# Modulation tiles split differently between two FFNs, and token places dealt out to partitions in steps of four

## What is computed

```python
def swiglu(x, w_gu, w_down):                       # d_ff 2816
    g, u = jnp.split(x @ w_gu, 2, axis=-1)
    return (jax.nn.silu(g) * u) @ w_down

def first_block(x, ...):
    h = x + 0.5 * rms_norm(swiglu(rms_norm(x, ffn1_pre_g), ffn1_w_gu, ffn1_w_down), ffn1_post_g)
    h = h + rms_norm(hybrid_mixer(rms_norm(h, mix_pre_g), ...), mix_post_g)
    return h + 0.5 * rms_norm(swiglu(rms_norm(h, ffn2_pre_g), ffn2_w_gu, ffn2_w_down), ffn2_post_g)

def second_block(x, c, ctx, c_ctx, w_mod, b_mod, ...):
    for layer in range(2):
        mod_l = jax.nn.silu(c) @ w_mod[layer] + b_mod[layer]          # w_mod[layer]: 1024 x 6144
        mod_c = jax.nn.silu(c_ctx) @ w_mod[layer] + b_mod[layer]
        ...                                         # token mixer, scaled and shifted by them
        f = hier_moe(tokens, w_rg, b_rg, w_re, b_re, w1, w3, w2)

def hier_moe(xf, ...):
    ...                                             # group, then the best 2 of its 8 experts
    xb = x_pad[row_tok].reshape(n_blocks, MOE_BLOCK, D)
    yb = (silu(xb @ w1[e]) * (xb @ w3[e])) @ w2[e]  # for each block, e its expert
    out = zeros.at[row_tok].add(yb * row_gate)
```

## Time and profile before

| | profiled execution |
|---|---|
| its own time | 3468.26 us |
| span, first to last instruction | 3466.1 us |
| mean granted clock of TensorE | 0.908 of full speed |
| PE busy | 2938.9 us, 85% |
| DVE busy | 1346.3 us, 39% |
| ACT busy | 791.8 us, 23% |
| POOL busy | 458.6 us, 13% |
| weight loads by SP (q1) | 571.69 MB, 42.5% of 16 DMA engines |
| loads by POOL (q0): modulation tiles, gathers | 104.88 MB, 8.9% |
| stores and loads by ACT (q10) | 29.53 MB, 2.3% |

### The profile page before, as it was taken

How to read it: one execution, slowest core, us unless ns; L and a number is a source line. 1 busy time by engine, 2 the same in 40 slices (tenths; PEclk the granted TensorE clock), 3 DMA queues, 4 the chain that set the end, 5 groups by cost and what they waited for, 6 DMA issues and landing times. The chain is left out here.

```text
span 3466.1 us, 37253 instructions
## 1 busy us (share of the span) xinstructions
PE 2938.9 (85%) x12832; PEld 1906.8 (55%) x12832; DVE 1346.3 (39%) x2365; ACT 791.8 (23%) x1392; POOL 458.6 (13%) x495
## 2 busy tenths in 40 slices
PE   5999978898998999879876888887497996888886
PEld 4777865476865888668653333333375843333333
DVE  4766584765116665421231111111548823111112
ACT  2222223253323222221220000000224611000000
POOL 0111221004410001031200000000320000000001
PEclk9999989857999999989987999999698997999998
DMA  4666621741223555411025999999110024999998
GB/s 155 223 219 224 219 87 51 244 156 38 95 103 105 193 193 198 160 38 61 13 104 209 403 391 395 395 395 360 65 62 12 0 99 159 408 407 395 409 411 305
DMA packets 151223, 706.97 MB, mean 204 GB/s; under 512 B 16368, under 2 KB 49520, under 8 KB 85744
## 3 DMA queue, kind: packets, MB, share of 16 engines
q1 hardware_dynamic: 106160, 571.69, 42.5%
q0 software_dynamic: 31280, 104.88, 8.9%
q10 hardware_dynamic: 13712, 29.53, 2.3%
HBM read 671.96 MB, written 53.74 MB: 209 GB/s over the span
## 5 line engine op out<-in xcount | busy, mean ns | idle before, releaser
L817 PE MATMUL bank<-big 128*64 128x512 f32 x1040 | 495.0, 623 | 122.0 <-DMA big<-in_w 119.7
L820 PE MATMUL bank<-big 128*64 128x512 f32 x1040 | 497.6, 625 | 0.0
L1790 DVE TENSOR_TENSOR big<-big,bank 64x512 f32<-64x512 f32 x65 | 44.9, 691 | 932.1 <-ACT big L1229 932.1
L817 PEld LDWEIGHTS bank<-big 128*64 128x64 f32 x1040 | 140.5, 143 | 443.1 <-issue 441.1
L832 PE MATMUL bank<-big 128*64 128x512 f32 x1040 | 270.5, 668 | 44.5 <-DVE big L1794 44.5
L1528 DVE SCALAR_TENSOR_TENSOR tabs<-tabs,tmp 128x1024 f32<-128x1024 f32 x160 | 195.8, 1234 | 170.5 <-DMA tabs<-in_wm 169.4
L543 PE MATMUL bank<-act_low 128*128 128x512 f32 (+1 forms) x480 | 166.0, 362 | 47.9 <-POOL u_split L2073 25.5
L543 PE MATMUL bank<-u_split,w_high 128*128 128x512 f32 x448 | 181.0, 404 | 8.6 <-ACT w_high L1095 8.6
L2088 POOL DMA_DIRECT2D tabs<-in_wm x160 | 84.9, 530 | 761.8 <-DVE tabs L1528 761.1
L543 PE MATMUL bank<-act_high,w_high 128*128 128x512 f32 x438 | 176.0, 402 | 10.8 <-POOL u_split L2112 10.8
L832 PEld LDWEIGHTS bank<-big 128*64 128x64 f32 x1040 | 79.2, 153 | 187.4 <-issue 186.1
(11 more groups left out here) (336 smaller groups left out, 5470.1 us busy)
## 6 DMA issues: line engine op xcount, KB each, us to landing
big<-in_w SPq DMA_DIRECT2D x402, 1024.0 KB
slot<-in_w SPq DMA_DIRECT2D x100, 1024.0 KB, 4.9
tabs<-in_wm POOLq DMA_DIRECT2D x160, 512.0 KB, 4.9
yb<-zeros SPq DMA_DIRECT2D x2, 14336.0 KB, 66.8
slot<-in_wd SPq DMA_DIRECT2D x16, 1408.0 KB, 7.3
yb<-big ACTq DMA_DIRECT2D x130, 128.0 KB, 7.0
rows<-big ACTq DMA_DIRECT2D x10, 512.0 KB, 2.6
lat<-in_x SPq DMA_DIRECT2D x1, 2048.0 KB, 10.6
```

Of the source, the lines that this page charges most:

```text
L817: ga = nc.tensor.matmul(bank[0][lo, :], xT[:, 4 * c + k, :], wslot[c][:, k * EF:(k + 1) * EF], **flags)
L820: mm = nc.tensor.matmul(bank[0][hi, :], xT[:, 4 * c + k, :], wslot[2 + c][:, k * EF:(k + 1) * EF], **flags)
L1790: nc.vector.tensor_tensor(hmul[MB:2 * MB, :], hsil[MB:2 * MB, :], bank[0][MB:2 * MB, :], ALU.mult).then_inc(q["h_ready"], 1)
```

## The change

The change has two parts.

*Modulation.* `MOD_SPLIT` is 81: the first FFN does 81 tiles, five in each round and 26 in its down product. The second does the other 15 of c first and then the 64 of c_ctx: five in each of rounds 0, 1, 2 and 4 to 10, none in round 3, 29 in its down product. `crow` is loaded with c again before the second FFN; behind round 2 ACT waits for 96 tiles done, loads c_ctx, and takes its silu behind round 3 (`MOD_SWITCH`), and DVE waits for that at round 4. The loads on POOL stay 160, one for each tile in the order in which they are done.

*Places.* `at_place` compares with a constant row `spread` instead of `count`, whose entry for partition q is q div 4 + 16 (q mod 4). So place 0 lies on partition 0, place 1 on 4, place 15 on 60, place 16 on 1, and so on. The block's results lie in `yb` by partition, so the position by which a token's row is gathered at the end becomes row + 3 place - 63 (place div 16), computed in six more operations on DVE. The gather itself, the weight loads and the products are not edited.

```diff
--- before.py
+++ after.py
@@ -68,8 +68,10 @@
 
 
 MOD_TILES = 6 * D // P
-MOD_OF = {1: [2 * t for t in range(2 * MOD_TILES)], 2: [2 * t + 1 for t in range(MOD_TILES + 2 * KT)]}
-MOD_ROUND = {1: 6, 2: 4}
+MOD_SPLIT, MOD_SWITCH = 2 * MOD_TILES - 15, 3
+MOD_OF = {1: [2 * t for t in range(MOD_SPLIT)],
+          2: [2 * t for t in range(MOD_SPLIT, 2 * MOD_TILES)] + [2 * t + 1 for t in range(MOD_TILES + 2 * KT)]}
+MOD_ROUND = {1: [5] * 11, 2: [5] * MOD_SWITCH + [0] + [5] * (10 - MOD_SWITCH)}
 
 DENSE = [("gu1", 22, 11), ("down1", 8, 2), ("xbr", 4, 2), ("q1", 4, 2), ("kv1", 2, 1),
          ("gate", 4, 2), ("merge", 16, 8), ("out1", 4, 2), ("gu2", 22, 11), ("down2", 8, 2),
@@ -93,7 +95,7 @@
         ("norm_mix", 16), ("norm_ffn", 16), ("conv_w2", 12), ("q_g", 1), ("k_g", 1), ("b_mod", 192),
         ("sinks1", 16), ("sinks2", 16), ("route_b", 2 * TT * ROUTE)]
 CONSTS = [("ident", 128), ("ones", 128), ("swap1", 128), ("swap2", 128), ("headsum", 128), ("before", 128),
-          ("mask1", 256), ("mask2", 384), ("eps", 1), ("gdesc", NG), ("edesc", NE), ("tri_lt", NE), ("tri_le", NE), ("count", max(TABW, MB)), ("tok", TT), ("thr", 16)]
+          ("mask1", 256), ("mask2", 384), ("eps", 1), ("gdesc", NG), ("edesc", NE), ("tri_lt", NE), ("tri_le", NE), ("count", max(TABW, MB)), ("spread", MB), ("tok", TT), ("thr", 16)]
 DFT = [("cs_d", 2 * P), ("c_ctx", 2 * C), ("s_ctx", 2 * C), ("c_lat", 4 * S), ("s_lat", 4 * S)]
 
 
@@ -276,6 +278,7 @@
         col = part(rt + 2096 + TABW + 1, [8])
         pos_f = part(rt + 2200, [2, 2, TT])
         place = part(rt + 2200 + 4 * TT, [2, TT])
+        place_f = part(rt + 2200 + 6 * TT, [2, 2, TT])
         used = part(rt + 2096, [TABW + 1])[0:MB, 0:TABW]
         at_place = part(m0 + 2 * D, [2 * TT, MB])
         in_block = part(m0 + 2 * D + 2 * TT * MB, [2 * TT, TABW])
@@ -399,7 +402,7 @@
 
         def mods_in_down(n):
 
-            left = len(MOD_OF[n]) - GU_ROUNDS * MOD_ROUND[n]
+            left = len(MOD_OF[n]) - sum(MOD_ROUND[n])
             return [left // (KT - 1) + (T < left % (KT - 1)) if T < KT - 1 else 0 for T in range(KT)]
 
 
@@ -1149,6 +1152,12 @@
                     for j in range(2):
                         act.wait_ge(scaled_ready, FT * (n - 1) + 2 * i + j + 1)
                         nc.scalar.activation(act_high[:, 2 * i + j, :], tmp[:, j, :], ACT.Copy).then_inc(ah_ready, 1)
+                    if n == 2 and i == MOD_SWITCH - 1:
+                        act.wait_ge(mod_done, 2 * MOD_TILES)
+                        act.dma_start(crow, d["crow"][1]).then_inc(crow_loaded, 16)
+                    if n == 2 and i == MOD_SWITCH:
+                        act.wait_ge(crow_loaded, 16 * 3)
+                        nc.scalar.activation(crow, crow, ACT.Silu).then_inc(crow_ready, 1)
                 ffn_high(n, 4 * GU_ROUNDS + 2)
                 sqrt_table()
                 r0 = plan[f"down{n}"][0]
@@ -1339,7 +1348,7 @@
                 merge_round(i)
             merge_round(KT - 1, last=True)
             act.wait_ge(mrg_ready, 8)
-            act.dma_start(crow, d["crow"][1]).then_inc(crow_loaded, 16)
+            act.dma_start(crow, d["crow"][0]).then_inc(crow_loaded, 16)
             sqrt_table()
             r0 = plan["out1"][0]
             for T in range(KT):
@@ -1554,9 +1563,10 @@
                 low(n, 3)
                 rsqrt(S)
                 dve.wait_ge(crow_ready, n)
-                per = MOD_ROUND[n]
                 for i in range(GU_ROUNDS):
-                    done = FT * (n - 1) + 2 * i
+                    done, per = FT * (n - 1) + 2 * i, MOD_ROUND[n][i]
+                    if n == 2 and i == MOD_SWITCH + 1:
+                        dve.wait_ge(crow_ready, 3)
 
                     def gate(j):
                         dve.wait_ge(full[j], r0 + 1 + i)
@@ -1575,9 +1585,9 @@
                     if i > 0:
                         low(n, 4 * i + 2)
                         low(n, 4 * i + 3)
-                    mods(2)
+                    mods(min(per, 2))
                     gate(1)
-                    mods(per - 3)
+                    mods(max(per - 3, 0))
                     up(0)
                     low(n, 4 * i + 4)
                     low(n, 4 * i + 5)
@@ -1586,7 +1596,7 @@
                         dve.wait_ge(ah_ready, done + j + 1)
                         nc.vector.tensor_tensor(act_low[:, 2 * i + j, :], tmp[:, j, :], act_high[:, 2 * i + j, :].bitcast(F32),
                                                 ALU.subtract).then_inc(act_ready, 1)
-                    mods(1)
+                    mods(min(per, 1))
                 low(n, 4 * GU_ROUNDS + 2)
                 for T, count in enumerate(mods_in_down(n)):
                     if T > 1:
@@ -1763,12 +1773,24 @@
 
                 dve.drain()
                 blk, row = pos_f[:, 1, :, 0:nt], pos_f[:, 0, :, 0:nt]
-                nc.vector.tensor_copy(pos_u[:, :, 0:nt], row)
                 nc.vector.scalar_tensor_tensor(place[:, :, 0:nt], blk, -float(MB), row, ALU.mult, ALU.add)
                 dve.drain()
+                sixteenth, part_of = place_f[:, 0, :, 0:nt], place_f[:, 1, :, 0:nt]
+                nc.vector.tensor_scalar(sixteenth, place[:, :, 0:nt], 15.5, None, ALU.is_gt)
+                for limit in (31.5, 47.5):
+                    dve.drain()
+                    nc.vector.scalar_tensor_tensor(sixteenth, place[:, :, 0:nt], limit, sixteenth, ALU.is_gt, ALU.add)
+                dve.drain()
+                nc.vector.scalar_tensor_tensor(part_of, place[:, :, 0:nt], 4.0, row, ALU.mult, ALU.add)
+                dve.drain()
+                nc.vector.tensor_tensor(part_of, part_of, place[:, :, 0:nt], ALU.subtract)
+                dve.drain()
+                nc.vector.scalar_tensor_tensor(part_of, sixteenth, -63.0, part_of, ALU.mult, ALU.add)
+                dve.drain()
+                nc.vector.tensor_copy(pos_u[:, :, 0:nt], part_of)
                 for t in range(nt):
                     for x in range(2):
-                        nc.vector.tensor_scalar(at_place[:, 2 * t + x, :], const("count")[:, 0:MB], place[:, x, t:t + 1], None, ALU.is_equal)
+                        nc.vector.tensor_scalar(at_place[:, 2 * t + x, :], const("spread"), place[:, x, t:t + 1], None, ALU.is_equal)
                         nc.vector.tensor_scalar(in_block[:, 2 * t + x, :], const("count")[:, 0:TABW], pos_f[:, 1, x, t:t + 1],
                                                 const("tok")[:, t:t + 1], ALU.is_equal, ALU.mult)
                 dve.drain().then_inc(q["tab_in"], 1)
@@ -2187,6 +2209,8 @@
     out["edesc"] = np.tile(np.arange(NE, 0, -1), (P, 1))
     e = np.arange(NE)
     out["tri_lt"], out["tri_le"] = np.tile(e[:, None] < e, (P // NE, 1)), np.tile(e[:, None] <= e, (P // NE, 1))
+    at = np.arange(MB)
+    out["spread"] = np.tile(at // 4 + 16 * (at % 4), (P, 1))
     out["count"] = np.tile(np.arange(max(TABW, MB)), (P, 1))
     out["tok"] = 1 + p[:, None] + P * np.arange(TT)
     out["thr"] = np.tile(MB * np.arange(16), (P, 1))
```

## The result

The changed kernel takes 3443.82 us, the median of 5 runs (3441.28 to 3449.54), against 3470.47 of before in the same comparison; the ratio is 0.9931, with a 95% interval of 0.9915 to 0.9947. It is faster by 0.7%: the ratio puts the gain at 24 us (18 to 29), the two medians at 26.7. The forecast was 3458, 12.9 us faster, so the gain is about twice what was forecast. The range of 3442 to 3472 holds the result by 2 us; the forecast's own range, 3452 to 3472, does not.

The account below looks back on a forecast made before the run. PE was taken as the bound, waiting on weight splits in the first FFN and on expert weights in every block. Terms -26.8 + 2.9 + 11 = -12.9 us gave 3458; range 3442 to 3472, the forecast's own 3452 to 3472.

Parts of the forecast that it names:

- own best case: Whole kernel, low end of the forecast's own range: -29.1 + 2.9 + 7.3 = -18.9 us, giving 3452.
- Fifteen tiles moved: Both FFNs: -20.4 us of PE waits, -6.8 of half-clock stretches, +0.4 charged to the second FFN; sum -26.8 us.
- half-clock stretches: First FFN, behind three PE waits: granted clock 0.50 for 6.8, 3.4 and 3.4 us; 6.8 us to come back.
- Positions: DVE ahead of each layer's table: six more operations of 0.24 us in each of two layers, uncovered, +2.9 us.
- Places: Expert blocks' gathers: steps of four put 33 more rows on the fullest engine, at 0.33 us each, +11 us.
- high end: Price of a row in the gathers: pace 16.96 against 16.44 for 4 rows against 2.8, 0.43 us each, 14.2 us.
- low end: Price of a row in the gathers, from the queue's share of 16 engines: 0.22 us each, 33 rows, 7.3 us.
- The dealing does nothing: Gathers: rows are short beside 6 MB of weights, only their sum counts; -23.9 us, 3447; chance 0.2.
- Eight engines fall behind together: Expert blocks: 40 us lost, total +16, 3487; decided above 0.38 us a block; chance 0.12.
- Spreads the load: Gathers: engines hold four neighbouring partitions, about 62 + 33 rows less on full ones, -21 us, total 3426; chance 0.08.

Follow-up runs that it names:

- count: Modulation tiles moved as in the change, positions computed behind the table, place p on partition p as before; 3435.55 us, ratio 0.9905 to the kernel before.
- four: Same instructions as count, only the constant row differs: the change's dealing in steps of four; 3442.52 us, ratio 0.9936 to the kernel before.
- two: Same instructions as count, only the constant row differs: places dealt in steps of two; 3428.73 us, ratio 0.9889 to the kernel before.
- crowd: Same instructions as count, only the constant row differs: a dealing that fills the same first partitions in every block; 3444.68 us, ratio 0.9941 to before.

## Why the prediction was right, and where it was not

The sign and the mechanism of the larger part held, but the gain came out about twice as large as forecast. Two of the terms were mis-sized, both by some 4 us or more and both towards too small a gain, so the errors added up. That the range holds the result is partly luck: its lower end of 3442 was put there to take in a rival that turned out false, and the forecast's own best case was 3452.

**Fifteen tiles moved: forecast -26.8, measured -31.2 with the unread row, -34.7 without it.** The steps of the sum hold in the trace. Waits of 20.4 us were to go, and 20.7 went. 6.8 us were to come back from half-clock stretches, half of the 13.6 us that the granted clock was 0.50; no run shows this term by itself, but the stretch is 28.7 us shorter, so 8.0 came back beside the waits, at a granted clock of 0.99 instead of 0.97. The second FFN was charged 0.4 and lost 0.2. What the sum lacked, 4 to 8 us, lies outside these steps. The prediction called 29.1 us a bound, the difference of the two FFNs in one execution. But the first FFN of before takes another time in each execution (21.1 and 24.0 us of waits in two traces of the same kernel), and the trace it was read from was not a long one: from PE's first product to the last of the first FFN it took 416.6 us, the second trace 418.8, and the eight traces with the tiles moved 386.8 to 388.0. Of the 1.2 us ahead of the first FFN, 1.0 is the constants' load, which the change does edit. The rest of the gap is not placed by any trace.

**Positions: forecast +2.9, measured 4.5 in the traces, not resolved in the runs.** The six operations cost 1.80 - 0.24 = 1.56 us a layer, as worked out (1.46). The sum overlooked what the longer wait does to PE. The table's product and the transposes behind it in layer 0, before and after:

```profile
1839.21 2.81 PE L793 MATMUL bank<-big 128*64 128x57 f32 x24 [9.24 <-DVEq L1774]
1841.95 1.35 PE L764 MATMUL bank<-consts,ar_u 128*128 128x128 f32 x8
```

```profile
1808.98 2.81 PE L796 MATMUL bank<-big 128*64 128x57 f32 x24 [10.73 <-DVEq L1796]
1811.72 1.97 PE L767 MATMUL bank<-consts,ar_u 128*128 128x128 f32 x8
```

PE stood 10.73 us instead of 9.24, and eight transposes then took 1.97 us instead of 1.35, the next eight 1.97 instead of 1.09. The windows of these transposes, before and after:

```profile
1842.00:1845.60 3.60, 2.39 (x17) 1.92 (x16) 0.42 (x2) 1.08 (x2) 0.00 (x0) 0.93 0.09 36
...
1811.80:1817.00 5.20, 3.86 (x16) 3.06 (x16) 0.42 (x2) 1.21 (x3) 0.00 (x0) 0.50 0.25 101
```

Before the change the granted clock rose during them (0.93 on average), after it the whole stretch is at 0.50. The four kernels with the positions behind the table have the rise again, and 85.7 to 85.8 us up to the first gather, as before, where the change has 88.8. The first gather waits for the rows that the transposes put out. So layer 0 lost 3.0 us, not 1.5, and layer 1 lost 1.5. From `place` to the first gather of layer 0 all four traces with the positions ahead of the table have 19.4 us, the other ten 16.4 to 16.5. In the runs the positions can't be told from nothing: steps of four with them behind the table took 3442.5 us (3440.0 to 3447.8), the change 3443.8 and 3444.0.

**Places: forecast +11, measured +4 to +7.** This is the term that was priced too high. No run shows its 33 rows more on a fullest engine, nor the 4 rows against 2.8 of its high end, since no trace names the engine of a packet: both are the author's estimate, with an engine for each group of four partitions. What the runs show is the number of rows among the first 16 packets (12.6, 7.6, 15.1 and 6.2 for count, four, two and crowd) and what each dealing took. The price was put at the middle of 0.22 and 0.43 us a row. The medians of count and four differ by 7.0 us, 0.22 a row, the low end; layer 1's blocks lost 5 to 6 us in the traces; and on the moved tiles and on the old ones dealing and positions together cost 8.3 and 8.6, which leaves 4 for the dealing if the positions cost the 4.5 of the traces. Only the ratios of count and four, 10.7 us apart, come near the forecast. Why the high end was too high is not shown. It divided the layers' difference in pace by rows, as if the layers differed in nothing else.

**The rivals.** "The dealing does nothing" named 3447, the nearest figure, and is nonetheless refuted by layer 1's pace and by the four dealings: it took the move 4 us or more too small and left out a dealing that costs 4 to 7, and the two errors cancel. "Eight engines fall behind together", with 0.38 us a block as its point of decision, did not come: layer 1's blocks lost 0.17 us each, and layer 0's pace with steps of four (16.92 to 17.06 in five traces) is that of count (16.94 to 17.06 in seven). "Spreads the load" fell with the 7.0 us that steps of four cost against count. Its price was also miscounted: by its own terms, four neighbouring partitions on an engine, 50 + 21 = 71 rows would come off the fullest ones, not 62 + 33, so 16 us and not 21.

**The checks named in advance.** The waits are gone but for 0.4 us, no half-clock stretch stands in the first FFN, the stretch is 342.9 us where about 345 was said, and behind the first two rounds a round takes 21.8 us on average where 21.7 was said: these held. Missed were no wait over 0.5 us in the second FFN (there is one of 0.9) and 16.8 us for layer 1's pace (it is 16.61). The prediction also said that 10 to 12 of the first 16 packets of a 20-row gather would still be rows. In this trace it is 8 (8 to 10 in the five with steps of four), and 8 of the 20 used places lie on the partitions 0, 2, ..., 30.

## What to carry to other kernels

Side work on an engine that others wait for can be harmless or costly by its place in the round: here the same six tiles, with one of them later, gained 26 us. Its amount still counts where it piles up, as at the end of that kernel's down product. A piece that must wait for its own load belongs behind the work on which the critical engine waits. Where a gather uses only some of its partitions, try several dealings of the places with the same instructions: against the plain order, steps of two were worth 6.8 us here by the medians, and the change's steps of four cost 4 to 7. And before an edit is judged by its time, run the kernel with only its change of layout, since two effects of 8 us can cancel to a clean "no change".

## What was not expected of the hardware

A row of 64 fp32 constants that nothing reads, 256 bytes a partition ahead of other tiles, made the kernel before 8.4 us faster (0.9964 to 0.9983), and made no difference that could be told once the first FFN's waits were gone (0.9902 against 0.9909). In the traces the constants land 1.0 us sooner with it. Whether the rest comes from the addresses of the tiles or from that earlier start was not tried; the 4 KB packets of the tile loads between 80 and 300 us take 188 ns on average in the first trace of before and in that with the row.

The longer wait of PE was paid twice in layer 0: behind 10.73 us of idle time instead of 9.24 the granted clock over the transposes was 0.50 instead of 0.93, and the first gather came 3.0 us later instead of 1.5.
